# Gate's 16 low-rank columns in fp32 on four column groups, and the small products of the projection stage in another order over two PSUM tensors

## What is computed

```
proj = einsum('bld,dc->blc', rmsnorm(x) * norm_mix, w_in[l])      # 1024 -> 3344 columns
p_gla, p_rwkv = proj[..., :1552], proj[..., 1552:]
q, k, v, g, glr = split(p_gla, (256, 256, 512, 512, 16))          # glr: the 16 low-rank columns
gate_logit = glr @ gla_gate_w2[l] + gla_gate_b[l]                 # 16 -> 256
log_a = log_sigmoid(gate_logit) / 16
xs = p_rwkv + mu * (previous_row(p_rwkv) - p_rwkv)
xr, xk, xv, xw, xa, xg = split(xs, (512, 512, 512, 64, 64, 128))
w_raw = w0 + tanh(xw) @ w2;   a = sigmoid(a0 + xa @ a2);   g = sigmoid(xg) @ g2
kk = xk * k_k;  kk = kk / max(norm(kk per head of 64), 1e-12);  k = xk * (1 + (a - 1) * k_a)
bonus = sum(r * k * r_k per head) * v
```

## Time and profile before

| | us |
|---|---|
| median of 3 runs (lowest, highest) | 1833.07 (1832.45, 1834.79) |
| time of the profiled execution | 1832.12 |
| its span, first to last instruction | 1830.4 |
| mean granted clock of TensorE, share of full speed | 0.975 |
| PE busy, PE weight loads busy | 1727.9 (94%), 1663.7 (91%) |
| DVE busy, ACT busy, POOL busy | 924.6, 665.6, 574.2 |

### The profile page before, as it was taken

How to read it: one execution, slowest core, us unless ns; L and a number is a source line. 1 busy time by engine, 2 the same in 40 slices (tenths; PEclk the granted TensorE clock), 3 DMA queues, 4 the chain that set the end, 5 groups by cost and what they waited for, 6 DMA issues and landing times.

```text
span 1830.4 us, 42294 instructions
## 1 busy us (share of the span) xinstructions
PE 1727.9 (94%) x19081; PEld 1663.7 (91%) x19081; DVE 924.6 (51%) x1367; ACT 665.6 (36%) x1004; POOL 574.2 (31%) x303
## 2 busy tenths in 40 slices
PE   5889999997999999999997999999889999999996
PEld 5778989996999999999996898999789999999995
DVE  4536843443656613666544676343345663166642
ACT  4324335544343312333242433445434332133322
POOL 3323320111434443344332333011133444344430
PEclk8989999998999999999998999999899999999998
DMA  4212210000232322323321223000022223222321
GB/s 124 70 35 69 81 54 9 4 4 7 81 91 83 94 80 73 88 84 91 90 78 36 64 74 87 9 3 4 3 64 82 81 81 96 78 82 81 94 79 54
DMA packets 218021, 116.33 MB, mean 64 GB/s; under 512 B 7108, under 2 KB 216178, under 8 KB 217842
## 3 DMA queue, kind: packets, MB, share of 16 engines
q1 hardware_dynamic: 216854, 111.15, 21.4%
q10 hardware_dynamic: 988, 2.48, 0.4%
HBM read 110.09 MB, written 3.53 MB: 62 GB/s over the span
## 4 chain that ended last, share of the span: by engine, by line
PE 91%; DVE 3%; ACT 3%; POOL 1%; issue 1%; DMA 0%; ACTq 0%; DVEq 0%; POOLq 0%
PE ps L533 35%; PE ps L534 35%; PE ps L538 2%; PE ps L708 2%; PE ps L712 2%; PE ps L670 2%; PE ps L704 1%; PE ps L683 1%; PE ps L828 1%; PE ps L812 1%; POOL wlo L462 1%; PE ps L747 1%; PE ps L774 1%; PE ps L871 1%; PE ps L880 1%
## 5 line engine op out<-in xcount | busy, mean ns | idle before, releaser
L462 POOL TENSOR_TENSOR wlo<-raw,whi 128x1024 fp32r<-128x1024 f32 (+1 forms) x190 | 513.5, 2703 | 873.1 <-ACT whi L1016 872.9
L1016 ACT ACTIVATE whi<-raw 128x1024 fp32r<-128x1024 f32 (+1 forms) x190 | 211.7, 1114 | 724.5 <-PE ps L534 706.0
L533 PE MATMUL ps<-xh,whi 128*128 128x288 f32 x1136 | 339.8, 299 | 11.3 <-POOL wlo L462 8.1
L534 PE MATMUL ps<-xh,whi 128*128 128x288 f32 x1136 | 337.5, 297 | 0.0
L533 PE MATMUL ps<-xl,whi 128*128 128x288 f32 x1136 | 336.8, 296 | 0.0
L534 PE MATMUL ps<-xl,whi 128*128 128x288 f32 x1136 | 336.6, 296 | 0.0
L533 PE MATMUL ps<-xh,wlo 128*128 128x288 f32 x1136 | 335.8, 296 | 0.0
L534 PE MATMUL ps<-xh,wlo 128*128 128x288 f32 x1136 | 334.9, 295 | 0.0
L533 PEld LDWEIGHTS ps<-xh,whi 128*128 128x128 f32 x1136 | 216.0, 190 | 13.0 <-POOL wlo L462 8.6
L534 PEld LDWEIGHTS ps<-xl,whi 128*128 128x128 f32 x1136 | 215.8, 190 | 0.0
L534 PEld LDWEIGHTS ps<-xh,whi 128*128 128x128 f32 x1136 | 215.5, 190 | 0.3
(11 more groups left out here) (256 smaller groups left out, 3334.7 us busy)
## 6 DMA issues: line engine op xcount, KB each, us to landing
raw<-in_ffn_w_up SPq DMA_DIRECT2D x88, 512.0 KB, 3.8
raw<-in_w_in SPq DMA_DIRECT2D x54, 512.0 KB, 3.8
raw<-in_ffn_w_down SPq DMA_DIRECT2D x32, 704.0 KB, 4.6
raw<-in_w_out SPq DMA_DIRECT2D x16, 512.0 KB, 3.6
xin<-in_x_prompt SPq DMA_DIRECT2D x4, 512.0 KB, 6.1
out<-yout ACTq DMA_DIRECT2D x4, 512.0 KB, 2.6
out<-RW SPq DMA_DIRECT2D x16, 64.0 KB, 2.2
g<-in_rwkv_g SPq DMA_DIRECT2D x2, 256.0 KB, 2.8
```

Of the source, the lines that this page charges most:

```text
L462: e.tensor_tensor(wlo[s][:, 0:width], raw[s][:, 0:width], whi[s][:, 0:width].bitcast(F32), ALU.subtract).then_inc(w_lo[s], 1)
L533: e.matmul(acc(out)[:, 0], lhsT, rhs[:, 0:HT], start=start, stop=stop)
L534: return e.matmul(acc(out)[:, 1], lhsT, rhs[:, HT:TOK], start=start, stop=stop)
L1016: e.activation(whi[s][:, 0:width], raw[s][:, 0:width], ACT.Copy).then_inc(w_hi[s], 1)
```

## The change

The 16 columns of `glr` no longer travel in a tile of 128. Their weights are loaded by a transfer of their own into `wlr` (128 x 8 x 32, zero in the upper 16 of each 32), DVE multiplies them by the norm's gains, and behind tile 1 PE makes 16 plain fp32 matmuls of 32 output columns by 288 tokens (`rank`): the 8 blocks of 128 inputs are spread over four groups of 32 columns of the array, so that four partial sums come to lie at partitions 0, 32, 64 and 96 of `PS[2]`. DVE's `low_rank` scales them into `G[:, 7]`. `gw2` holds four copies of `gla_gate_w2`, so that the logits' products, now 128 rows deep, add the four partial sums. `turn` loses its extra turn, and all tiles alternate between the slots.

The small products are reordered. `w` and `a` of one p come together behind the tiles 3 to 6, `w` into `PS[2]` from partitions 0 to 63 and `a` into `PS[3]` from partitions 64 to 127, their matmuls interleaved. `n` goes behind the tiles 7 to 10 into `PS[2]` and `PS[3]` by turns and waits for the `mx` two before it. The logits go behind tile 12, `b` into `PS[2]` behind the GLA tiles 2, 5, 8, 10, and `g` into `PS[3]` behind 4, 6, 9, 11. DVE's and ACT's orders follow: DVE makes the logits before the last `shifted`, the whole of a pair's vectors between two rows, and `Plast` pair by pair; ACT copies `g` as it comes, and `act("g3")`, `dve("bv3")` are waited for inside the chunk loop instead of ahead of it. SP waits for the constants ahead of the parameter rows instead of behind them.

```diff
+LR = 16
+LR_GROUPS = 4
+PRE_PE = ["lr", "w0", "a0", "w1", "a1", "w2", "a2", "w3", "a3", "n0", "n1", "n2", "n3", "l0", "l1",
+          "b0", "g0", "b1", "g1", "b2", "g2", "b3", "g3"]
...
                     if it == 0:
+                        sp.wait_ge(consts, N_CONSTS)
+                        sp.wait_ge(pre_pe, l * len(PRE_PE))
+                        sp.dma_start(wlr[:, :, 0:LR], w_in[l].rearrange("(k p) c -> p k c", p=P)[:, :, GLA_COLS - LR:GLA_COLS])\
+                          .then_inc(wlr_loaded, 16)
...
-                        sp.dma_start(gw2[LR_AT:LR_AT + 16, :], gla_gate_w2[l]).then_inc(small_loaded, 16)
-
-                in_tile(0, turn(0, l, PAIRS["gla"], False), GLA_COLS - 16 - LR_AT)
+                        for c in range(LR_GROUPS):
+                            sp.dma_start(gw2[32 * c:32 * c + LR, :], gla_gate_w2[l]).then_inc(small_loaded, 16)
...
+            const(e.memset(wlr[:, :, :], 0.0))
...
+                def rank(out, weights, rhs, first, last):
+
+                    for c in range(LR_GROUPS):
+                        mm = e.matmul(out[32 * c:32 * c + 32], weights[c], rhs[c], start=first, stop=last)
+                    return mm
...
+                    if t == 1:
+                        pe.wait_ge(wlr_scaled, l + 1)
+                        pe.wait_ge(n_rs, 2 * l * NORMS + 1)
+                        for b in range(2):
+                            for k in range(KT // LR_GROUPS):
+                                ks = range(k, KT, KT // LR_GROUPS)
+                                mm = rank(acc(PS[2])[:, b], [wlr[:, kt, :] for kt in ks],
+                                          [x[:, kt, b * HT:(b + 1) * HT] for kt in ks], k == 0, k == 1)
+                        mm.then_inc(pre_pe, 1)
                     if 3 <= t < 7:
...
-                            act(f"w{p - 1}")
-                        wide(PS[2], w2a2[0:64, p * P:(p + 1) * P], R[0:64, 12]).then_inc(pre_pe, 1)
+                            act(f"a{p - 1}")
+                        for tt in (slice(0, 512), slice(512, TOK)):
+                            ws = e.matmul(PS[2][:, tt], w2a2[0:64, p * P:(p + 1) * P], R[0:64, 12, tt], start=True, stop=True)
+                            as_ = e.matmul(PS[3][:, tt], w2a2[64:128, p * P:(p + 1) * P], R[64:128, 12, tt],
+                                           start=True, stop=True)
...
                     if 7 <= t < 11:
                         p = t - 7
-                        act(f"a{p - 1}" if p else "w3")
-                        wide(PS[2], w2a2[64:128, p * P:(p + 1) * P], R[64:128, 12]).then_inc(pre_pe, 1)
-                    if 5 <= t < 9:
-                        p = t - 5
                         act(f"sq{p}")
-                        if p == 0:
-                            pe.wait_ge(par_ready, (l + 1) * 4)
+                        if p < 2:
+                            act("a3")
+                            pe.wait_ge(consts, N_CONSTS)
                         else:
-                            dve(f"mx{p - 1}")
-                        wide(PS[3], mean64[:, :], G[:, 8 + p]).then_inc(pre_pe, 1)
-
-                dense(0, turn(0, l, PAIRS["gla"], False), xh, xl, KT)
+                            dve(f"mx{p - 2}")
+                        wide(PS[2 + p % 2], mean64[:, :], G[:, 8 + p]).then_inc(pre_pe, 1)
+                    if t == 12:
+                        for q in range(2):
+                            dve(f"mx{2 + q}")
+                            wide(PS[2 + q], gw2[:, q * P:(q + 1) * P], G[:, 7]).then_inc(pre_pe, 1)
...
-                    if t in (2, 5, 8, 9):
-                        p = {2: 0, 5: 1, 8: 2, 9: 3}[t]
+                    if t in (2, 5, 8, 10):
+                        p = {2: 0, 5: 1, 8: 2, 10: 3}[t]
                         dve(f"rk{p}")
...
+                        wide(PS[2], mean64[:, :], G[:, 8 + p]).then_inc(pre_pe, 1)
+                    if t in (4, 6, 9, 11):
+                        p = {4: 0, 6: 1, 9: 2, 11: 3}[t]
...
+                        wide(PS[3], g2[:, p * P:(p + 1) * P], R[:, 13]).then_inc(pre_pe, 1)
...
-                act("g3")
-                dve("bv3")
+                dve("ke1")
...
+                e.tensor_tensor(wlr[:, :, 0:LR], wlr[:, :, 0:LR],
+                                gains[:, at:at + KT].unsqueeze(2).broadcast_to([P, KT, LR]), ALU.mult).then_inc(wlr_scaled, 1)
...
+                    if t == 1:
+                        low_rank()
...
-                    if 6 <= t < 10:
-                        key_norm(t - 6)
+                    if 7 <= t < 11:
+                        key_norm(t - 7)
...
-                dv.wait_ge(tile_done[0], turn(0, l, PAIRS["gla"], False) + 1)
-                e.tensor_tensor(by_half(R[LR_AT:P, 12, :]), acc(PS[0])[LR_AT:P], by_half(nrs[LR_AT:P, :]), ALU.mult)\
-                 .then_inc(psum_free[0], 1)
+                logits(0)
+                logits(1)
                 shifted(RT - 1)
                 nk(0)
                 b_vector(0)
```

More of the change, by code:

```diff
@@ L160, in program @@
         gw2 = sb("gw2", [P, GK])
+        wlr = sb("wlr", [P, KT, 2 * LR])
         r_k64 = sb("r_k64", [P, NP])
@@ L468, in _ @@
                     for s in range(2):
-                        split(s, turn(s, l, PAIRS["rwkv"] + it, False), KT * P)
-                split(0, turn(0, l, PAIRS["gla"], False), KT * P)
+                        split(s, turn(s, l, PAIRS["rwkv"] + it), KT * P)
                 for it in range(0, GT // 2):
@@ L1087, in decays @@
                     e.activation(cum[:, p, :], cum[:, p, :], ACT.Exp, scale=-KAPPA).then_inc(pre_act, 1)
-                ac.wait_ge(tile_done[0], turn(0, l, PAIRS["rwkv"], False) + 1)
-                split(0, turn(0, l, PAIRS["rwkv"], False) + 1)
+                ac.wait_ge(tile_done[0], turn(0, l, PAIRS["rwkv"]) + 1)
+                split(0, turn(0, l, PAIRS["rwkv"]) + 1)
                 norm(l * NORMS)
@@ L1094, in _ @@
                     if t > 0:
-                        tile(s, turn(s, l, PAIRS["rwkv"] + t // 2, False))
+                        tile(s, turn(s, l, PAIRS["rwkv"] + t // 2))
                     ac.wait_ge(r_scaled, n + 1)
@@ L1137, in _, with copy_gate, bonus_bias @@
                 decays(2)
+                def copy_gate(p):
+                    dve(f"pl{p}")
+                    pe_(f"g{p}")
+                    e.activation(gate[:, p, :], PS[3][:, 0:TOK], ACT.Copy).then_inc(pre_act, 1)
+                def bonus_bias(p):
+                    dve(f"bv{p}")
+                    e.activation(T[p][:, 0:TOK], T[p][:, 0:TOK], ACT.Identity, bias=pcol("ln_b", p)).then_inc(pre_act, 1)
                 for t in range(0, GT):
@@ L1158, in _ @@
                         e.activation(cg[:, q, :], cg[:, q, :], ACT.Exp, scale=1.0 / 16).then_inc(pre_act, 1)
-                    if t in (8, 11):
-                        for p in (range(2) if t == 8 else range(2, 4)):
-                            dve(f"bv{p}")
-                            e.activation(T[p][:, 0:TOK], T[p][:, 0:TOK], ACT.Identity, bias=pcol("ln_b", p))\
-                             .then_inc(pre_act, 1)
+                    if t in (4, 6, 9):
+                        copy_gate((4, 6, 9).index(t))
                     if t >= 8:
@@ L1166, in _ @@
                         e.activation(G[:, t, :], G[:, t, :], ACT.Silu).then_inc(silu_done, 1)
-                    if t >= 10:
-                        for p in ((0,), (1, 2, 3))[t - 10]:
-                            if p == 0:
-                                dve("pl")
-                            pe_(f"g{p}")
-                            e.activation(gate[:, p, :], PS[2 + p % 2][:, 0:TOK], ACT.Copy).then_inc(pre_act, 1)
+                    if t == 7:
+                        bonus_bias(0)
+                        bonus_bias(1)
+                    if t == 10:
+                        bonus_bias(2)
+                bonus_bias(3)
+                copy_gate(3)
                 def step(sem_, order, j, name):
@@ L1592, in _ @@
                 k_tilde(0)
-                gla_row(1)
-                logits(0)
-                logits(1)
-                gla_row(2)
                 a_tilde(0)
                 r_tilde(0)
+                last_decays(0)
+                gla_row(1)
                 nk(1)
                 b_vector(1)
+                rk(1)
+                b_tilde(1)
+                k_tilde(1)
+                gla_row(2)
+                a_tilde(1)
+                r_tilde(1)
+                last_decays(1)
+                nk(2)
+                b_vector(2)
                 gla_row(3)
@@ L1633, in _ @@
                 gla_scaled(1)
-                e.tensor_copy(Plast[:, :, :], cum[:, :, C::CP]).then_inc(pre_dve, 1)
+                gla_row(11)
                 bonus(3)
-                gla_row(11)
                 def step(sem_, order, j, name):
```

100 lines of the change are left out of this document (46 added, 54 removed), and 12 rows, old and new, of tables (PRE_AC, PRE_DV).

## The result

| | before | after |
|---|---|---|
| median of 4 runs, us (lowest to highest) | 1833.93 (1832.45 to 1835.19) | 1761.83 (1760.66 to 1763.12) |
| time of the profiled execution | 1832.12 | 1763.12 |
| span of the profiled execution | 1830.4 | 1761.1 |
| mean granted clock of TensorE | 0.975 | 0.985 |

The ratio is 0.9607, 95% interval 0.9591 to 0.9624: 72 us less. The forecast was 1771 us with a range of 1763 to 1786. The direction and most of the size were right; the time lies 9 us under the forecast and 1.2 us outside the range.

What follows compares the result with a forecast made beforehand. PE was taken to set the end of each layer's projection stage, 209.8 and 210.4 us. Terms summed to 179.6 us per stage; 62.4 us saved left 1769.7, so 1771 us was forecast, range 1763 to 1786.

Steps and rivals of the forecast that it cites:

- The new product: Low-rank product behind tile 1, 16 matmuls of 288 columns: taken as 4.4 us per layer, bounds 2.3 to 8.0.
- chain of records: In the low-rank product and pairs: a matmul's second record waits for its first; n matmuls take n + 1 record times.
- w with a: Projection stage: eight products at 1.42 us become four pairs on two row groups at 1.85, gaining 4.0 us per layer.
- full overlap: Rival for the low-rank product and pairs: 2.3 and 1.4 us, 8 us less, 1763 us; chance 0.07.
- The tile and its hole: Projection stage: the extra low-rank tile, 6.34 us, and the 5.67 us hole before the first GLA tile go.
- The `mx` waits and the clock behind them: Between tiles 6 and 9: PE's waits for DVE's `mx` and the clock's fall go, 16.0 us per layer.
- The end: Last tile to `gram`: one `g` product instead of three, 2.5 us of waiting gone; layer 0's chunk loop gains 1.7.
- DVE at its limit at the first row: GLA part: DVE needs about 12.6 us against 12.7, 0.3 charged per layer; late-row rival 1775 to 1787 us, chance 0.12.
- The start: At launch: POOL clears one more tile and PE's first instruction waits for POOL, costing 0.3 us.
- ACT's sigmoids: At tiles 4 to 6: PE needs the previous tile's sigmoid of `a`; ACT has 3.0 us per tile and fits 8.2.
- the rivals of the mean waits and of the clock: Projection stage: waits move to ACT's sigmoids, 1803 us, chance 0.03; clock falls to 1.2 GHz, near 2131 us, chance 0.02.

Runs made afterwards that it cites:

- run 3: The changed kernel with the whole low-rank product on one group of 32 columns instead of four, logits 32 deep: 1774.45 us.
- run 2: The kernel before with only the low-rank part of the change (extra tile replaced by the 16 matmuls, logits 128 deep): 1812.44 us against 1832.14.
- run 1: The kernel before with only the four `n` products moved one tile later on PE, behind tiles 6 to 9: 1799.38 us against 1832.14.
- run 5: The changed kernel with two more DVE operations of 576 columns ahead of the first GLA row in each layer: 1764.19 us.

## Why the prediction was right in most of its mechanisms and wrong in one

**The step that failed is "The new product", and its chain of records, which the step "w with a" took over.** It said that a matmul's second record waits for its first and only the next matmul's first can run beside it, so that n matmuls take n + 1 record times and "Four groups gain nothing over two in that order". The runs showed almost full overlap in its place: the first records of a pair begin 0.01 us apart and the second ones together, and four groups bring the new product's records from 7.95 to 2.15 us (run 3). The new product measured 2.28 us for 4.4 and a pair 1.43 for 1.85. That is 2 x (2.1 + 1.7) = 7.6 us of the time. The Trainium skill, page "TensorEngine Tiling (Array Packing)", section "Theoretical Speedup", gives up to fourfold for a dimension of 32 or less; the trace agrees, with 7.95 to 2.15 us, a factor of 3.7.

The error was in reading. Four matmuls on two groups had taken 0.59 us; I read 0.54 for a chain and 0.05 for the rest. It can as well be 0.43 for full overlap and 0.16 for a switch of shape, and the row can't tell them apart. I had a price for a switch, 0.33 for both ends, and put it on the new product, but not on that row. The forecast gave full overlap 0.07, and put the lower end of the range on exactly that case, with nothing for any other term that was a little high and nothing for the spread of the runs.

**Term by term.** With the two measured prices the sum is 24 x 6.34 + 2.3 + 5.7 + 15.3 = 175.5 us, and both stages are 175.35.

- The tile and its hole: right, shown by run 2 (19.7 us measured, 19.5 expected of it).
- The `mx` waits and the clock behind them, 16.0 a layer: right, shown by run 1 (32.8 measured, 32 expected).
- The end, 2.5 a layer and 1.7 of clock in layer 0: the waits are gone. From the chunk loop's first matmul in layer 0 to ACT's first table load of the line that is L1235 before and L1264 after it was 32.10 us and is 30.45, so the 1.7 is right. Layer 1 took 30.45 already before, at clock 1.00, behind the same waits (1.5 and 0.9 us): such waits bring the clock down there at times and not always, and the forecast was right to count layer 0 alone.
- DVE at its limit at the first row: the count gave about 12.6 us against 12.7. Measured it is 149.29 + 0.75 - 137.79 = 12.25, and PE begins the tile that needs it at 150.29, 12.5 after tile 13. The 0.3 us charged was not paid; run 5 shows that the limit is real.
- The start: 0.3 forecast. Tile 1 ends at 47.15 for 45.7, 1.4 later. 0.9 of that is there when the scaled input begins, a time that spreads by 0.8 us over kernels with the same start. The other 0.5 lies in tile 1 and goes with the clock: from 36.5 to 47.0 us it was 0.80 before and 0.70 here.
- ACT's sigmoids are not late, and the clock is 1.00 through both stages: the rivals of the mean waits and of the clock did not come.

The spans differ by 69.3 us, 6.9 more than the 62.4 forecast, and the medians by 72.1. Some 2 us of the 9.2 have no mechanism behind them: the forecast put the median 0.95 us above the profiled execution, and the changed kernel's lies 1.3 below it, since the profiled one was the slowest of the four, with a span 1.0 to 2.9 us longer than the others. That execution, 1763.12 us, would have been just inside the range; the step above failed all the same.

## What to carry to other kernels

When small products stand between large ones on TensorE, give each consumer a whole tile of time before the next product needs its buffer; here moving four products by one tile was worth 32.8 us, a third of it clock. Small fp32 products that use different rows or columns of the array cost here as much as one, as long as no more than two for the same part stand in a row. And when a row is explained by a rate plus an overhead, charge the overheads priced elsewhere to it before reading a mechanism out of what is left.

## What the runs showed of the hardware that was not expected

- Plain fp32 matmuls on separate row or column groups overlap almost fully: 32 records of 288 columns took 7.95 us on one group of 32 columns and 2.15 on four. Two 64-deep products of 576 columns together cost 1.43 us, one alone 1.42.
- Their order in the queue mattered only from the third in a row on. Cost of the same 16 matmuls on four groups, from tile 1 to 2 less 6.34: by turns 2.28 us, two in a row 2.31, three in a row 3.80, four in a row 5.26 (58.41 - 46.81 - 6.34). A queue that stops when a third matmul comes for a group that has two gives 2.3, 2.3, 3.7 and 5.1. That such a queue is the cause is inferred from these four times; one of them was forecast.
- A wait of 2.1 us ahead of the chunk loop was followed by granted clock 0.63 and 0.60 over the next 3.5 us in the two layers, while a wait of 1.08 us in the projection stage was not (clock 1.00). In the kernel before, two waits of 1.5 and 0.9 us at the same place were followed by 0.67 over 5.2 us in layer 0 and by 1.00 in layer 1, so the length of a wait alone does not decide it.
